# Adaptive modulation of the first 512 channels ahead of the rest, with its sums on TensorE, and the setup's pieces, transfers and parameters in another order

## The chip, the core and the metric

The kernel runs on one core of one Trainium2 chip. Its engines are TensorE (PE; its weight loads are shown apart as PEld), VectorE (DVE), ScalarE (ACT), GpSimd (POOL) and SyncE (SP, which here only issues transfers). The metric is the device time of one execution in microseconds, lower is better. All times below are of the program as a whole or offsets from the start of the profiled execution.

## The reference, cut to what matters here

```python
c_act = jax.nn.silu(c)                                          # (1, 1024)
shift, scale, gate = jnp.split(c_act @ w_ada[l] + b_ada[l], 3, axis=-1)
h = rms_norm(x, norm_w[l]) * (1.0 + scale[:, None, :]) + shift[:, None, :]
proj = h @ w_in[l]                                              # (2048, 1024) @ (1024, 8768)
# ... gated causal depthwise convolution of 31 taps, LayerNorm; latent attention of 8 heads;
# merge by sigmoid gates, w_out, residual, RMSNorm
```

Everything is float32: x is 2048 tokens by 1024 channels, `w_ada` 1024 by 3072. The change concerns `shift`, `scale` and `h`, that is, what must be there before the first large product can start.

## The kernel before

Four phases follow each other: front, value, attention, output. Only the first 117 us of the front phase are touched. There `h` is built, transposed (channels on partitions, tokens along the row), and split into a high part `h_hi` and a remainder `h_lo`, since every large product is done as three matmuls (`split3`, L52 to L54). The 2048 tokens are four chunks (g = 0 to 3) of 512, the 1024 channels eight tiles (t = 0 to 7) of 128. One **piece** is one (g, t): four 128x128 transposes on TensorE (`turn_x`, L911), the eviction `x * gain + shift` on ScalarE (`turn_out`, L429), the cast to `h_hi` (L695) and the subtraction to `h_lo` (L697) on VectorE, and then six matmuls of 512 columns on TensorE, for the first two column tiles of `w_in` at once. 32 pieces run in the order g outer, t inner. `X_BANKS` names the PSUM bank of each piece's transposes; TensorE turns piece n + 4 after the matmuls of piece n, with a hole after pieces 4 to 7, because banks are still taken (pieces 8 to 11 are turned together after piece 7).

Ahead of the first piece stand `shift` and `gain`. Their 2048 columns of `w_ada` come in four blocks of 512 (j = 0, 1 shift, j = 2, 3 scale), 2 MB each in two halves. For each block VectorE does 8 operations (L669, L672) that multiply the rows by silu(c) and add them up, and `ada_products` (L892) sums over the partitions on TensorE by 8 matmuls of one column against a constant matrix. After all four blocks VectorE makes `shift` and `gain` in four small operations (L683 to L690), and ScalarE, which waits for them (`ada_vec`), can evict the first piece.

x arrives in four groups of four row tiles. For each, ScalarE squares four tiles (`square_x`, L418) and takes the root (L422), VectorE inverts (`invert_x`, L657), GpSimd scales the four tiles (`scale_x`, L581), and TensorE may turn. The squares of later groups stand behind the evictions of pieces 0 to 11, the inversions behind pieces 3, 7 and 11. The two column tiles of `w_in` are split on ScalarE (L411) and GpSimd (L586). When a chunk's pieces are done, ScalarE evicts the two results (`evict`, L434), for g = 0 to 2 between later pieces. After piece 31 ScalarE and GpSimd split column tile 2, and TensorE goes on with it.

All input transfers are on SyncE's queue in this order: c; x group 0; blocks 0 and 1 of `w_ada`; seven small rows of parameters and the 31 x 1024 taps of the convolution (into `prm` and `taps`); `w_in` tiles 0 and 1; blocks 2 and 3; x groups 1 to 3. TensorE turns the parameters (L923, L925) after the products of block 1.

## Time and profile before

| what | us |
|---|---|
| median of 3 runs (2698.75 to 2700.75) | 2699.91 |
| the profiled execution | 2704.03 |
| its span, first to last instruction | 2702.2 |
| TensorE busy in it | 2586.2 (96%) |
| VectorE busy in it | 1755.0 (65%) |
| mean granted TensorE clock | 0.984 |

The times are of one profiled execution, 4.1 us above the median of the runs. "PE busy" counts matmuls in flight. The granted clock is 1.00 at 2.4 GHz and 0.50 at 1.2 GHz; before TensorE's clock first changes in this execution the column reads 1.00 whatever the level was, and the durations of the matmuls tell the level. In timeline rows "x16" counts matmul records: a float32 product of one column leaves two records, one of the 8 per block each.

### The profile page before, as it was taken

The page shows a single profiled execution, that of the slowest core. Times are in us where ns is not written, and L with a number is a line of the kernel's source. Part 1 is how long each engine was busy: PE and PEld are TensorE (multiplying, and loading weights), DVE is VectorE, ACT ScalarE, POOL GpSimd, SP SyncE. Part 2 cuts the span into 40 slices and gives each one's busy share as a digit, 9 for nine tenths or more (in the row PEclk, how much of TensorE's full clock was granted, in tenths as well). Part 3 has the DMA queues.
Part 4 walks back from the last instruction along what each step waited for, and adds up shares of the span by engine and source line. Part 5 has one row for each costly group of instructions (what it writes and reads, how often), then busy time and mean ns, then how long its engine had stood idle before and what let it go on. Part 6 is the DMA issues. An engine that isn't in the chain of part 4 may idle for free. (4 is left out here: it accounts for less than half of the span.)

```text
span 2702.2 us, 32620 instructions
## 1 busy us (share of the span) xinstructions
PE 2586.2 (96%) x12186; PEld 2127.4 (79%) x12186; DVE 1755.0 (65%) x2073; ACT 850.5 (31%) x1683; POOL 640.9 (24%) x592
## 2 busy tenths in 40 slices
PE   4989999999999999997899999999999999999998
PEld 4767888888888888786677877877878778888887
DVE  5777967979779789564277667667677622223442
ACT  3432111111111111232255555555555520201221
POOL 3132111111111111232032232232232320323422
PEclk8999999999999999999899999999999999999999
DMA  8053212122112121376923112112112164666542
GB/s 298 8 164 116 78 47 78 47 67 83 53 55 78 47 78 48 124 243 240 278 73 107 62 60 107 62 60 107 61 61 86 55 202 156 205 215 211 190 149 78
DMA packets 200833, 306.74 MB, mean 114 GB/s; under 512 B 18234, under 2 KB 119678, under 8 KB 190621
## 3 DMA queue, kind: packets, MB, share of 16 engines
q1 hardware_dynamic: 194604, 284.89, 32.1%
q0 software_dynamic: 6128, 20.45, 2.4%
q8 instruction: 70, 1.15, 0.2%
q14 instruction: 31, 0.25, 0.0%
HBM read 202.01 MB, written 103.28 MB: 113 GB/s over the span
## 5 line engine op out<-in xcount | busy, mean ns | idle before, releaser
L52 PE MATMUL ps_proj<-h_hi,w_hi 128*128 128x512 f32 x1696 | 670.6, 395 | 9.0 <-DVE h_lo L697 6.8
L54 PE MATMUL ps_proj<-h_hi,w_lo 128*128 128x512 f32 x1696 | 663.1, 391 | 0.0
L53 PE MATMUL ps_proj<-h_lo,w_hi 128*128 128x512 f32 x1696 | 663.0, 391 | 0.0
L812 DVE SCALAR_TENSOR_TENSOR acc<-u,taps_t,acc 128x2048 f32<-128x2048 f32 x240 | 629.0, 2621 | 8.5
L52 PEld LDWEIGHTS ps_proj<-h_hi,w_hi 128*128 128x128 f32 x1696 | 320.7, 189 | 77.9 <-issue 8.0
L53 PEld LDWEIGHTS ps_proj<-h_lo,w_hi 128*128 128x128 f32 x1696 | 320.7, 189 | 67.9 <-issue 2.5
L54 PEld LDWEIGHTS ps_proj<-h_hi,w_lo 128*128 128x128 f32 x1696 | 320.2, 189 | 67.4
L586 POOL TENSOR_TENSOR w_lo<-raw,w_hi 128x1024 fp32r<-128x1024 f32 x53 | 168.4, 3177 | 808.5 <-ACT w_hi L411 808.4
L1719 POOL TENSOR_SCALAR prob<-prob,rinv 128x512 f32<-128x512 f32 (+2 forms) x320 | 199.0, 638 | 352.3 <-DVE rinv L1670 352.1
L1675 DVE TENSOR_TENSOR pt_lo<-ps_t,pt_hi 128x512 fp32r<-128x512 f32 (+1 forms) x320 | 194.1, 609 | 96.8 <-ACT pt_hi L1594 93.1
L1594 ACT ACTIVATE pt_hi<-ps_t 128x512 fp32r<-128x512 f32 (+1 forms) x320 | 169.4, 532 | 237.6 <-PE ps_t L1500 237.6
L1652 DVE TENSOR_REDUCE nmax<-ps_ring 128x1 f32<-128x512 f32 (+3 forms) x288 | 174.6, 622 | 96.1 <-PE ps_ring L1485 78.0
L539 ACT ACTIVATE lat<-ps_proj 128x512 f32<-128x512 f32 x128 | 76.3, 598 | 493.6 <-PE ps_proj L54 429.2
L2005 DVE TENSOR_TENSOR o_y<-o_ps,o_g 128x512 f32<-128x512 f32 x64 | 43.9, 690 | 265.2 <-PE o_ps L54 201.2
L1586 ACT ACTIVATE prob<-ps_ring,nbias 128x512 f32<-128x512 f32 (+2 forms) x320 | 195.3, 625 | 37.5 <-DVE nbias L1658 33.1
L52 PE MATMUL o_ps<-o_a_hi,o_w_hi 128*128 128x512 f32 x512 | 199.8, 390 | 3.4 <-DVEq L1996 3.4
L53 PE MATMUL o_ps<-o_a_lo,o_w_hi 128*128 128x512 f32 x512 | 199.9, 390 | 0.0
L54 PE MATMUL o_ps<-o_a_hi,o_w_lo 128*128 128x512 f32 x512 | 199.8, 390 | 0.0
L1500 PE MATMUL ps_t<-ident,prob 128*128 128x128 f32 x1088 | 173.3, 275 | 14.9 <-POOL prob L1719 9.5
L1500 PEld LDWEIGHTS ps_t<-ident,prob 128*128 128x128 f32 x1088 | 131.4, 141 | 48.2 <-POOL prob L1719 12.2
L1515 PE MATMUL ps_o<-pt_hi,v_hi 128*128 128x512 f32 (+1 forms) x320 | 141.4, 442 | 0.7 <-DVE bg L1683 0.7
L1480 PE MATMUL ps_ring<-kn_hi,qn_hi 128*128 128x512 f32 (+2 forms) x320 | 125.3, 392 | 8.4 <-ACT prob L1586 5.0
(220 smaller groups left out, 4037.8 us busy)
## 6 DMA issues: line engine op xcount, KB each, us to landing
qlat<-qlat_dram SPq DMA_DIRECT2D x32, 1024.0 KB, 5.9
raw<-in_w_in_dram SPq DMA_DIRECT2D x52, 512.0 KB, 6.4
under_h<-in_w_ada_dram SPq DMA_DIRECT2D x8, 1024.0 KB, 11.2
ga_dram<-lat SPq DMA_DIRECT2D x8, 1024.0 KB, 5.0
gb_dram<-lat SPq DMA_DIRECT2D x8, 1024.0 KB, 5.0
agate_dram<-lat SPq DMA_DIRECT2D x8, 1024.0 KB, 5.0
conv_dram<-acc SPq DMA_DIRECT2D x8, 1024.0 KB, 3.9
bgate_dram<-lat SPq DMA_DIRECT2D x8, 1024.0 KB, 5.0
```

The costliest lines, as they stand in the source:

```text
L52: pe.matmul(out, wh, xh, start=first, stop=False)
L53: pe.matmul(out, wh, xl, start=False, stop=False)
L54: return pe.matmul(out, wl, xh, start=False, stop=last)
L586: pool.tensor_tensor(weights(tile)[1][:], raw[tile % 2][:], weights(tile)[0][:].bitcast(F32), ALU.subtract).then_inc(lo_made, 1)
L812: dve.scalar_tensor_tensor(acc[:], u[:, n:n + S], tap(n), acc[:], ALU.mult, ALU.add).then_inc(conv_tap if n < TAPS - 1 else conv_done, 1)
L1500: mm = pe.transpose(ps_t[:, n % 2, b * P:(b + 1) * P], prob[:, x:x + P], k.ident[:])
L1515: pe.matmul(out, v_hi[:, j, :], mh, start=(j == 0), stop=False)
L1586: act.activation(prob[:, x:x + width], ps[:, chunk_no[n, c] % RING, 0:width], ACT.Exp, bias=nbias[:, n:n + 1], accum_out=rsum[:, n, c:c + ...
L1594: act.activation(pt_hi[n % SLOTS][:, s], ps_t[:, n % 2, s], ACT.Copy).then_inc(t_hi, 1)
L1652: ins = dve.tensor_reduce(to, ps[:, chunk_no[n, c] % RING, 0:width], AX.X, ALU.max, negate=True)
L1675: dve.tensor_tensor(pt_lo[n % SLOTS][:, s], ps_t[:, n % 2, s], pt_hi[n % SLOTS][:, s].bitcast(F32), ALU.subtract).then_inc(t_lo, 1)
L1719: pool.tensor_scalar(prob[:, x:x + width], prob[:, x:x + width], rinv[:, n:n + 1], 1.0, ALU.mult, ALU.mult).then_inc(normed, 1)
```

## The change

It touches seven things in the front phase; nothing behind piece 31 differs.

1. Blocks of `w_ada` are taken in the order `ADA_COLS` = 0, 2, 1, 3: shift and scale of channels 0 to 511 first. Each half has a semaphore of its own.
2. For the first two blocks TensorE does the whole sum (`modulate`): 32 matmuls per block, each with 128x128 weights out of `w_ada` as it was loaded and one column of silu(c). The last two blocks keep the way of before, VectorE's part of them being put behind pieces 3 and 7, TensorE's (`ada_products`) behind the transposes after piece 3 and behind piece 7.
3. `shift` and `gain` are made in two halves (`shift_and_gain`), the second behind block 3.
4. `PIECES`: (0, 0 to 3), (1, 0 to 3), (0, 4 to 7), (1, 4 to 7), then chunks 2 and 3 as before. Piece 8 is the first that needs the second half of `gain`. `X_BANKS`, the squares, evictions and inversions are given by new tables.
5. VectorE scales two of four row tiles of x groups 2 and 3.
6. The small parameters and the taps are issued by GpSimd, and TensorE waits for all of them before the sums.
7. SyncE's order: c, x 0, block 0, `w_in` tiles 0 and 1, block 1, x 1, blocks 2 and 3, x 2 and 3.

```diff
-    X_BANKS = [[1, 5, 2, 6], [3, 7, 2, 6], [0, 4, 3, 7], [1, 5, 0, 4]]
+    ADA_COLS = [0, 2, 1, 3]
+    PIECES = ([(g, t) for half in range(2) for g in range(2) for t in range(half * KH, (half + 1) * KH)]
+              + [(g, t) for g in range(2, NC_) for t in range(KT)])
...
+    INVERT_AT = {3: 1, 10: 2, 16: 3}
...
+                for r, n, src in rows[1:]:
+                    pool.dma_start(prm[r:r + n, :], src.rearrange("o (t p) -> (o t) p", p=P)).then_inc(params_in, 16)
+                pool.dma_start(taps, k.conv_w.rearrange("o t c -> (o t) c")).then_inc(params_in, 16)
...
-                    for i in range(g * QB, (g + 1) * QB):
+                    for i in range(g * QB, (g + 1) * QB)[:QB // 2 if g > 1 else QB]:
...
+                def piece(n):
+                    g, t = PIECES[n]
...
+                    if n in INVERT_AT:
+                        invert_x(INVERT_AT[n])
+                        if INVERT_AT[n] > 1:
+                            scale_x(INVERT_AT[n])
...
+                shift_and_gain(0)
+                for n in range(KH):
+                    piece(n)
+                modulation(2)
+                for n in range(KH, 2 * KH):
+                    piece(n)
+                modulation(3)
+                shift_and_gain(1)
+                for n in range(2 * KH, N_PIECE):
+                    piece(n)
...
+                def modulate(j):
+                    for kh in range(2):
+                        pe.wait_ge(ada_in[j][kh], 16)
+                        for m in range(QB):
+                            for t in range(KH):
+                                at = kh * KH + t
+                                mm = pe.matmul(ps_ada[:, ADA_COLS[j] * QB + m:ADA_COLS[j] * QB + m + 1],
+                                               wada_at[j][kh][:, t, m * P:(m + 1) * P], k.cact[:, at:at + 1],
+                                               start=(at == 0 and m == 0), stop=(at == KT - 1 and m == QB - 1))
+                    mm.then_inc(ada_mm, 1)
...
-                ada_products(0)
-                for n in range(AHEAD):
-                    turn_x(n)
-                ada_products(1)
+                pe.wait_ge(cact_done, 1)
                 pe.wait_ge(params_in, 16 * len(rows))
...
-                ada_products(2)
-                ada_products(3)
+                modulate(0)
+                for n in range(AHEAD):
+                    turn_x(n)
+                modulate(1)
...
-                    held = n < KT and n >= KT - AHEAD
-                    if n == KT - 1:
-                        for m in range(KT, KT + AHEAD):
+                    if n == KH - 1:
+                        for m in range(KH, 2 * KH):
                             turn_x(m)
-                    elif not held and n + AHEAD < N_PIECE:
+                        ada_products(2)
+                    if n == 2 * KH - 1:
+                        ada_products(3)
+                    if KH <= n < N_PIECE - AHEAD:
                         turn_x(n + AHEAD)
```

TensorE before, from the second block's products on (`mean_mat` is the constant matrix, `lat` holds VectorE's sums, `ident` marks a transpose):

```order
L892 MATMUL ps_proj<-mean_mat,lat 128x1 x7
L923 MATMUL ps_proj<-ident,prm 128x68 [waits params_in]
L925 MATMUL ps_proj<-ident,lat 128x31 x8
L892 MATMUL ps_proj<-mean_mat,lat 128x1 [waits ada_step]
L892 MATMUL ps_proj<-mean_mat,lat 128x1 x7
```

and TensorE of the change, from the start of the phase (`cact` is silu(c), `under_h` where `w_ada` lands):

```order
L953 MATMUL ps_proj<-ident,prm 128x8 [waits c_in,consts]
L957 MATMUL ps_proj<-ident,prm 128x68 [waits params_in,cact_done]
L959 MATMUL ps_proj<-ident,lat 128x31 x8
L920 MATMUL ps_proj<-cact,under_h 128x1 [waits ada_in00]
L920 MATMUL ps_proj<-cact,under_h 128x1 x15
L920 MATMUL ps_proj<-cact,under_h 128x1 [waits ada_in01]
L920 MATMUL ps_proj<-cact,under_h 128x1 x15
L948 MATMUL ps_proj<-ident,u 128x128 [waits x_scaled]
```

The parameters moved to the front, and each of the first two blocks has 32 one-column matmuls where it had 8.

TensorE around the fourth piece (n = 3). Before, piece 3, the turning of piece 7, piece 4:

```order
L54 MATMUL ps_proj<-h_hi,w_lo1 128x512
L911 MATMUL ps_proj<-ident,u 128x128 [waits full_done]
L911 MATMUL ps_proj<-ident,u 128x128
L911 MATMUL ps_proj<-ident,acc 128x128 x2
L52 MATMUL ps_proj<-h_hi,w_hi0 128x512 [waits h_lo_done]
```

and in the change, where `under_h0` holds x group 1:

```order
L54 MATMUL ps_proj<-h_hi,w_lo1 128x512
L948 MATMUL ps_proj<-ident,under_h0 128x128 [waits params_sb,x_scaled]
L948 MATMUL ps_proj<-ident,under_h0 128x128 x3
L948 MATMUL ps_proj<-ident,under_h0 128x128 [waits full_done,x_scaled]
L948 MATMUL ps_proj<-ident,under_h0 128x128 x3
L948 MATMUL ps_proj<-ident,under_h0 128x128 [waits full_done,x_scaled]
L948 MATMUL ps_proj<-ident,under_h0 128x128 x3
L948 MATMUL ps_proj<-ident,under_h0 128x128 [waits full_done,params_sb,x_scaled]
L948 MATMUL ps_proj<-ident,under_h0 128x128 x3
L929 MATMUL ps_proj<-mean_mat,lat 128x1 [waits ada_step]
L929 MATMUL ps_proj<-mean_mat,lat 128x1 x7
L52 MATMUL ps_proj<-h_hi,w_hi0 128x512 [waits h_lo_done]
```

Between pieces 3 and 4 now stand 16 transposes that wait for the scaled x group 1, and 8 products that wait for VectorE's sums of block 2.

VectorE around its fourth piece. Before:

```order
L697 TENSOR_TENSOR h_lo<-wada_gate,h_hi 128x512 [waits h_hi_done]
L657 RECIPROCAL ss<-ss 128x4 [waits root_done]
L695 CAST h_hi<-wada_gate 128x512 [waits full_done]
L697 TENSOR_TENSOR h_lo<-wada_gate,h_hi 128x512 [waits h_hi_done]
L695 CAST h_hi<-wada_gate 128x512 [waits full_done]
```

and in the change:

```order
L705 TENSOR_TENSOR h_lo<-wada_gate,h_hi 128x512 [waits h_hi_done]
L664 RECIPROCAL ss<-ss 128x4 [waits root_done]
L679 TENSOR_SCALAR lat<-under_h0,cact 128x512 [waits ada_in21,ada_in20]
L679 TENSOR_SCALAR lat<-under_h0,cact 128x512
L682 SCALAR_TENSOR_TENSOR lat<-under_h0,cact,lat 128x512 [waits ada_step] x6
L703 CAST h_hi<-wada_gate 128x512 [waits full_done]
```

The eight operations of block 2 now stand between VectorE's pieces 3 and 4.

## Rows read from the trace of the kernel before

**Rows 1.** Busy time per stretch: each engine's, then granted clock, DMA share, GB/s
```profile
core 0: us, PE busy (x) PEld busy (x) DVE busy (x) ACT busy (x) POOL busy (x), PEclk, DMA share, GB/s
28.00:32.00 4.00, 3.81 (x31) 3.62 (x29) 0.65 (x1) 1.61 (x2) 3.37 (x2) 1.00 1.05 399
32.00:36.00 4.00, 0.00 (x0) 0.00 (x0) 1.39 (x3) 0.00 (x0) 1.27 (x1) 0.61 1.05 386
80.00:84.00 4.00, 3.82 (x12) 3.12 (x13) 3.22 (x7) 1.99 (x3) 0.00 (x0) 0.59 0.02 4
```
**Rows 2.** Timeline of TensorE: start, duration, what; in brackets idle before and releaser
```profile
20.17 3.57 PE L892 MATMUL ps_proj<-mean_mat,lat 128*128 128x1 f32 x16 [17.65 <-DVE lat L672]
25.51 0.69 PE L911 MATMUL ps_proj<-ident,u 128*128 128x128 f32 x2 [1.77 <-POOL acc L581]
...
28.98 2.10 PE L892 MATMUL ps_proj<-mean_mat,lat 128*128 128x1 f32 x16
...
31.13 0.68 PE L925 MATMUL ps_proj<-ident,lat 31*128 31x31 f32 x8
...
44.94 3.57 PE L892 MATMUL ps_proj<-mean_mat,lat 128*128 128x1 f32 x16 [1.83 <-DVE lat L672]
51.41 0.76 PE L52 MATMUL ps_proj<-h_hi,w_hi 128*128 128x512 f32 x1 [2.91 <-DVE h_lo L697]
...
80.18 0.50 PE L52 MATMUL ps_proj<-h_hi,w_hi 128*128 128x512 f32 x1 [2.48 <-DVE h_lo L697]
...
86.92 0.60 PE L911 MATMUL ps_proj<-ident,under_h 128*128 128x128 f32 x4
87.28 0.48 PE L52 MATMUL ps_proj<-h_hi,w_hi 128*128 128x512 f32 x1
...
88.75 0.60 PE L911 MATMUL ps_proj<-ident,under_h 128*128 128x128 f32 x4
...
110.91 0.38 PE L911 MATMUL ps_proj<-ident,part 128*128 128x128 f32 x2
...
117.92 1.99 PE L957 MATMUL ps_proj<-acc,mean_mat 128*128 128x512 f32 x4 [1.14 <-POOL w_lo L586]
```
**Rows 3.** Timeline of VectorE, blocks of `w_ada`, `gain`, an inversion, and two later operations
```profile
15.26 0.88 DVE L669 TENSOR_SCALAR lat<-under_h,cact 128x512 f32<-128x512 f32 x2 [15.26 <-DMA under_h<-in_w_ada_dram]
...
20.64 2.32 DVE L669 TENSOR_SCALAR lat<-under_h,cact 128x512 f32<-128x512 f32 x2 [0.43 <-DMA under_h<-in_w_ada_dram]
22.88 5.76 DVE L672 SCALAR_TENSOR_TENSOR lat<-under_h,cact,lat 128x512 f32<-128x512 f32 x6
...
40.82 4.06 DVE L672 SCALAR_TENSOR_TENSOR lat<-under_h,cact,lat 128x512 f32<-128x512 f32 x6
48.62 0.17 DVE L683 SCALAR_TENSOR_TENSOR shift<-ps_proj,prm_t 128x8 f32<-128x8 f32 x1 [3.74 <-PE ps_proj L892]
...
56.60 0.18 DVE L657 RECIPROCAL ss<-ss 128x4 f32<-128x4 f32 x1 [0.21 <-ACT ss L422]
...
115.67 3.28 DVE L713 TENSOR_SCALAR u<-u,freqs 128x2048 f32<-128x2048 f32 x1
...
130.55 1.23 DVE L719 TENSOR_SCALAR u<-u 128x2048 f32<-128x2048 f32 x1
```
**Rows 4.** Timeline of GpSimd: scaling of x group 0, and its first transfer
```profile
20.30 2.37 POOL L581 TENSOR_SCALAR u<-u,ss 128x1024 f32<-128x1024 f32 x2 [17.81 <-DVE ss L657]
22.66 2.80 POOL L581 TENSOR_SCALAR acc<-acc,ss 128x1024 f32<-128x1024 f32 x2
...
143.77 1.12 POOL L595 DMA_DIRECT2D u<-in_w_ada_dram  x1 [0.72 <-DMA trig_dram<-u]
```
**Rows 5.** Timeline of ScalarE, the first eviction
```profile
49.30 0.78 ACT L429 ACTIVATE wada_gate<-ps_proj,shift,gain 128x512 f32<-128x512 f32 x1 [19.06 <-DVE gain L690]
```
**Rows 6.** Timeline of SyncE's queue, the taps
```profile
13.05 0.25 SPq L334 DMA_DIRECT2D lat<-in_conv_w_dram  x1
```
**Rows 7.** DMA from 20 to 28 us, in 40 slices of 0.2 us
```profile
GB/s 312 233 207 169 202 202 159 128 54 41 23 38 123 97 105 187 292 361 328 333 317 302 156 77 28 20 10 20 23 20 23 31 172 123 92 61 110 317 338 420
```

More of the change, by code:

```diff
@@ L196, in front_phase @@
         params_in = sem("params_in")
-        ada_in = [sem(f"ada_in{j}") for j in range(ADA_J)]
+        ada_in = [[sem(f"ada_in{j}{kh}") for kh in range(2)] for j in range(ADA_J)]
         x_in = [sem(f"x_in{g}") for g in range(NC_)]
@@ L297, in _ @@
             def _(sp):
-                def row(r, n, src, landed):
-                    sp.dma_start(prm[r:r + n, :], src.rearrange("o (t p) -> (o t) p", p=P)).then_inc(landed, 16)
                 def load_x(g):
@@ L326, in store_part @@
                     sp.dma_start(dst[1], part_lo.bitcast(F32)).then_inc(part_lo_out, 16)
-                row(*rows[0], c_in)
+                sp.dma_start(prm[R_C:R_C + KT, :], k.c.rearrange("o (t p) -> (o t) p", p=P)).then_inc(c_in, 16)
                 load_x(0)
                 ada(0)
-                ada(1)
-                for r in rows[1:]:
-                    row(*r, params_in)
-                sp.dma_start(taps, k.conv_w.rearrange("o t c -> (o t) c")).then_inc(params_in, 16)
                 tile_weights(0)
                 tile_weights(1)
+                ada(1)
+                load_x(1)
                 ada(2)
                 ada(3)
-                for g in range(1, NC_):
-                    load_x(g)
+                load_x(2)
+                load_x(3)
                 sp.dma_start(freqs[:], k.freqs).then_inc(pos_in, 16)
@@ L688, in _, with shift_and_gain @@
-                dve.tensor_scalar_add(gain[:], gain[:], 1.0).then_inc(ada_vec, 1)
-                dve.wait_ge(ada_vec, 3)
-                dve.tensor_tensor(gain[:], gain[:], k.prm_t[:, R_NORM:R_NORM + KT], ALU.mult).then_inc(ada_vec, 1)
-                for n in range(N_PIECE):
-                    g, t = divmod(n, KT)
+                def shift_and_gain(half):
+                    t = slice(half * KH, (half + 1) * KH)
+                    of = lambda r: slice(r + half * KH, r + (half + 1) * KH)
+                    scale = float(D) if half else 1.0
+                    dve.wait_ge(ada_mm, 2 * (half + 1))
+                    dve.scalar_tensor_tensor(gain[:, t], ps_ada[:, of(KT)], scale, k.prm_t[:, of(R_BADA + KT)],
+                                             ALU.mult, ALU.add).then_inc(ada_vec, 1)
+                    dve.scalar_tensor_tensor(shift[:, t], ps_ada[:, of(0)], scale, k.prm_t[:, of(R_BADA)],
+                                             ALU.mult, ALU.add).then_inc(ada_vec, 1)
+                    dve.wait_ge(ada_vec, 4 * half + 1)
+                    dve.tensor_scalar_add(gain[:, t], gain[:, t], 1.0).then_inc(ada_vec, 1)
+                    dve.wait_ge(ada_vec, 4 * half + 3)
+                    dve.tensor_tensor(gain[:, t], gain[:, t], k.prm_t[:, of(R_NORM)], ALU.mult).then_inc(ada_vec, 1)
@@ L896, in turn_x @@
                 def turn_x(n):
-                    g, t = divmod(n, KT)
-                    b = X_BANKS[g][t % 4]
-                    if t == 0:
-                        pe.wait_ge(x_scaled, QB * (g + 1))
-                        if g == 1:
-                            pe.wait_ge(ada_vec, 2)
-                            pe.wait_ge(params_sb, 2)
-                        if g >= 2:
-                            pe.wait_ge(chunk_out, 2 * (g - 1))
-                    before = [m for m in range(n) if X_BANKS[m // KT][m % 4] == b]
+                    g, t = PIECES[n]
+                    b = X_BANKS[n]
+                    pe.wait_ge(x_scaled, QB * (g + 1))
+                    if b == 7:
+                        pe.wait_ge(params_sb, 2)
+                    if b == 3:
+                        pe.wait_ge(ada_vec, 6)
+                    if n >= 2 * KT and b % NC_ < 2:
+                        pe.wait_ge(chunk_out, 2 * (b % NC_ + 1))
+                    before = [m for m in range(n) if X_BANKS[m] == b]
                     if before:
```

62 lines of the change are left out of this document (30 added, 32 removed).

## The prediction, made before the changed kernel had run

> **What bounds the kernel now.** TensorE is busy for 96% of the span, so a change in the first 117 us moves the end by as much as it moves the point from which TensorE runs without waiting. I read the timeline of TensorE first [rows 2], and in it the waits in brackets: the three product groups with waits ahead (17.65 us, 1.83 us), 2.91 us ahead of the first large matmul at 51.41, 2.48 us ahead of the one at 80.18. Then the engine that ends each wait: VectorE's blocks of `w_ada` [rows 3], GpSimd's scaling [rows 4], ScalarE's first eviction at 49.30 [rows 5]. I call that moment T0, since the first `gain` ends there. Last, the granted clock by stretches [rows 1]. The reader is to see that up to T0 the sums over `w_ada` end last, and after it TensorE, which needs 1.83 us a piece with its four transposes (86.92 to 88.75). The last transposes end at 110.91 + 0.38 = 111.3, which is T0 + 62.0. Behind them follow four pieces, ScalarE's and GpSimd's split and tile 2 (the row at 117.92, [rows 2]); all of that hangs on the last piece by the same chain in both kernels, so I move it as a whole. I compare the moment at which the last transposes end, 111.3 before, and carry the difference to the end one to one.
>
> **Up to T0: what goes and what comes.** VectorE's eight operations for blocks 0 and 1 go (the second block took 2.32 + 5.76 = 8.1 us beside GpSimd, a block alone some 4.9). What comes instead is on TensorE: 32 one-column matmuls a block for 8. The price is in the row of the same form, 128x128 weights and one column: 16 records in 3.57 us at the low level of the clock (20.17 and 44.94), 2.10 at 28.98, when the clock had mostly risen [rows 2]. Four such groups back to back are 14.0 us at the low level and 7.0 at the high one.
>
> When can the first begin? Block 0 was complete at 15.26 [rows 3]; at 386 GB/s [rows 1] its second megabyte takes 2.7 us, so its first half is there at 12.5. But TensorE now first waits for all parameters. GpSimd is free from 20.30 - 17.81 = 2.5 us [rows 4]. It issues eight transfers, each between 0.25 us (SyncE's price of the taps, [rows 6]) and 1.12 (GpSimd's for 512 KB, [rows 4]): done between 4.5 and 11.5. Landing is the unknown. Where the taps were in flight before, the stream fell to 10 to 31 GB/s for eight slices on end, 1.6 us [rows 7]; at 20 GB/s the taps' 127 kB are 6.3 us. So the parameters are there between 7 and 20 us. I take 13.5, near the middle, since GpSimd has nothing else to do. With 0.9 us for turning them (0.68 for the taps at 31.13, and one transpose more), the sums start at 14.4; bounds 13.4 and 20.9.
>
> The Trainium skill (DMA: Bandwidth & Descriptors, "Why a DMA increments its semaphore by 16 and not by 1") says that the number of DMA engines of a transfer must divide its slowest dimension, which for 31 rows is one engine, and that GpSimd's software path gives some copies all 16 nevertheless. By the first the taps land late (the rival below), by the second early; rows 7 fit the first for SyncE's queue, and no row shows GpSimd's.
>
> First block: 14.4 + 14.0 = 28.4. Transposes of pieces 0 to 3: 3.5 us at the low level (25.51 to 28.98), 31.9. Scaled x is there at 25.5 at the latest. Second block: before, the clock was high from the end of these transposes (the faster group at 28.98) to 32.9 (mean 0.61 in 32 to 36, [rows 1]), 3.9 us. If it does the same again, 3.9 us do the work of 7.8 and the other 6.2 go at the low level: 10.1 us, 42.0. If not, 45.9. From the last product to the first eviction 49.30 - 48.51 = 0.8 (44.94 + 3.57 = 48.51). **T0 is 42.8 instead of 49.3, a lead of 6.5 us.**
>
> The Trainium skill (TensorE: Matmul & The Clock Gate, "Part 4: PE-mode transpose") says that transposes don't count as work that raises the clock. Here the clock rose right behind 3.5 us of nothing but transposes, so the row speaks against it; by the page the lead would be 2.6 us.
>
> The transfers' new order by itself gives nothing: block 1 was complete at 20.64 [rows 3], and 1.05 MB of `w_in` ahead of it, even at the 156 GB/s that are the mean of rows 7, add 6.7: it is there before the second block's sums start at 31.9.
>
> **From T0 on: 62.0 us before.** Pieces 0 to 3 are as before up to the inversion, which ends at T0 + 7.5 (56.60 + 0.18 - 49.30). Then GpSimd scales x group 1 and VectorE does block 2. That very pair stood at 20.30: GpSimd took 5.2 us and VectorE 8.1 [rows 3, 4]. So x 1 is scaled at 12.7 and block 2 summed at 15.6. TensorE is through with four pieces at about 9.8 and waits; before, it had pieces 4 to 7 to work on in this time. Sixteen transposes: 3.5 us at the low level, 16.2; products of block 2: 19.7 (both at the high level: 17.4). I take the low level, as an idle of 2.48 us ahead of 80.18 was enough for 0.59 in 80 to 84 [rows 1, 2].
>
> Pieces 4 to 7 with three turnings: 4 x 1.83 - 0.46 = 6.9, and 1.7 more for a start at the low level as long as the one at 80 to 84, 3.3 us of 4 [rows 1]: 28.3. Block 3 on VectorE is hidden: 15.6 + 4 x 1.15 + 4.9 = 25.1. Its products take 1.9, `gain` 0.8: ScalarE's piece 8 can start at T0 + 31.0. Its first matmul is 2.1 later (51.41 - 49.30), 33.1. Pieces 8 to 27, twenty of 1.83, are 36.6: 69.7. The half scaling on VectorE comes twice, behind pieces 10 and 16: two operations of 1024, alone 0.6 each, beside GpSimd up to 1.6 (2048 took 1.23 and 3.28, [rows 3]), in a stretch where VectorE needs 1.15 of the 1.83 us anyway. Each also waits for the root and its partner on GpSimd. I take 4 us of TensorE's waits for both (bounds 1 and 7), and 0.9 for the clock after the idle ahead of piece 8. **Sum: 74.6, that is 12.6 more than before**; bounds 67 (no low level, no waits) and 78.
>
> In all 12.6 - 6.5 = **+6.1 us**. The profiled execution of 2704.03 would be 2710.1; put on the median of the runs, 2699.91, it is 2706.0.
>
> **Rivals.** (1) *The clock rises inside the first block's sums.* Then 4.0 us at the low level, 5.0 at the high one, transposes 1.8 and the second block 7.0: T0 = 33.0, a lead of 16.3, and the products in the second half are shorter by 3.3: 9.3 - 16.3 = -7.0, 2692.9, faster. It decides as soon as the rise comes before the middle of the first block. Against it: the group at 44.94 was done at the low level, 1.83 us behind another of its kind, and after the group at 28.98 the clock was low by 32.9. For it: no row has such matmuls for more than 3.6 us on end. The Trainium skill (TensorE: Matmul & The Clock Gate, "Part 1: The HAM clock gate") has sustained matmuls raise the clock and makes no exception for one-column ones; this rival is what it would give. 12%.
> (2) *The taps are late.* Parameters at 20 us, sums from 20.9, 6.5 later than taken: 2712.5. For it rows 7, against it that GpSimd's queue need not spread like SyncE's. 27%.
> (3) *The waits after T0 are mostly covered.* Sum 67 to 69 instead of 74.6, the change then within 2 us of nothing: about 2699. It needs the scaling and block 2 to interleave better than the pair at 20.30 did. 18%.
> (4) *The transposes don't raise the clock for the second block.* T0 = 46.7, 2709.9. 10%.
> The forecast, lead 6.5 and 12.6 given back, has 33%, with a range of its own from 2701 to 2711.
>
> **How the numbers follow.** 0.2% is 5.4 us, about what a measurement of this kernel can tell. Slower than 2705.3: over half of the forecast's case, nearly all of (2) and (4), together 0.55. Faster than 2694.5: most of (1), a little of (3), 0.12. Between: 0.33. The range leaves out the far half of (1) below, and (2) with the upper bound of the waits above: 2694 to 2717.
>
> **What would show it.** Right: the one-column matmuls of the first block spread over about 14 us with a start near 14; the first eviction at 40 to 44; TensorE idle for some 3 us behind piece 3 and again ahead of piece 8; VectorE's block 2 taking 8 us; waits ahead of the matmuls of pieces 11 and 17; the transposes' end at 114 to 120. Wrong: a first block done in 9 us or less (rival 1), a start of the sums near 20 (rival 2), pieces 4 to 7 right behind piece 3 (rival 3). The whole would be wrong if something behind piece 31, where nothing is changed, took up or gave back what the first 117 us lose.

## The result: 8.9 us slower, by the mechanism that was forecast

| | before | changed |
|---|---|---|
| median of the runs (7 each, same chip) | 2699.91 us (2698.66 to 2703.29) | 2708.92 us (2702.73 to 2716.21) |
| ratio to before, 95% interval | | 1.0033 [1.0023, 1.0043] |
| profiled execution, its span | 2704.03, 2702.2 us | 2710.15, 2708.3 us |
| first eviction, T0 [rows 5] | 49.30 | 41.07 |
| end of the last transposes [rows 2] | 111.3 | 118.8 |
| first matmul of tile 2 [rows 2] | 117.92 | 125.42 |
| from there to the end of the span | 2584.3 | 2582.9 |

The 8.9 us are the ratio to before, put on 2700 us; the two medians differ by 9.0. TensorE starts 8.2 us earlier on the large products and is 7.5 us late when the last x is turned. The 1.4 us that come back behind it can't be read as an effect of the change: that code is the same in all fourteen kernels of this study, and it took between 2579.7 and 2586.0 us in their profiled executions.

### The changed kernel up to T0

TensorE's timeline of the changed kernel (columns as in [rows 2]; x64 are the matmul records of one block's sum):

```profile
11.44 0.35 PE L957 MATMUL ps_proj<-ident,prm 68*128 68x68 f32 x1 [8.72 <-DMA lat<-in_conv_w_dram]
11.71 1.06 PE L959 MATMUL ps_proj<-ident,lat 31*128 31x31 f32 x8
12.70 13.81 PE L920 MATMUL ps_proj<-cact,under_h 128*128 128x1 f32 x64
...
28.97 0.56 PE L948 MATMUL ps_proj<-ident,u 128*128 128x128 f32 x2
29.37 0.38 PE L948 MATMUL ps_proj<-ident,acc 128*128 128x128 f32 x2
29.59 10.77 PE L920 MATMUL ps_proj<-cact,under_h 128*128 128x1 f32 x64
43.19 0.77 PE L52 MATMUL ps_proj<-h_hi,w_hi 128*128 128x512 f32 x1 [2.83 <-DVE h_lo L705]
```

The first block is the low level from end to end: 13.81 us for 64 records is 0.216 us each, against 0.223 in [rows 2] at 44.94. The transposes behind it go from 0.63 us to 0.38 a pair at 29, and the second block has some 3 us at the high level. GpSimd issues the parameters in 0.51 to 0.73 us each, the taps last, at 5.96, and these are there at 11.4. The stretch of 10 to 31 GB/s [rows 7] is gone: from 20 to 28 us the stream stays at 386 to 388 GB/s. Busy time per stretch (columns as in [rows 1]), first before, then changed:

```profile
20.00:24.00 4.00, 3.57 (x16) 3.48 (x16) 3.56 (x5) 0.00 (x0) 3.69 (x4) 1.00 0.74 180
24.00:28.00 4.00, 2.49 (x12) 2.49 (x13) 4.00 (x6) 0.51 (x1) 1.46 (x1) 1.00 0.56 133
```
```profile
20.00:24.00 4.00, 4.00 (x20) 4.00 (x21) 0.00 (x0) 0.00 (x0) 4.00 (x3) 1.00 1.05 386
24.00:28.00 4.00, 4.00 (x20) 4.00 (x21) 0.00 (x0) 0.00 (x0) 0.76 (x1) 1.00 1.05 388
```

### The changed kernel behind T0

ScalarE's first eviction, T0, and TensorE again, the interruptions of its pieces:

```profile
41.07 0.78 ACT L431 ACTIVATE wada_gate<-ps_proj,shift,gain 128x512 f32<-128x512 f32 x1 [21.56 <-DVE gain L697]
```
```profile
54.29 3.68 PE L948 MATMUL ps_proj<-ident,under_h 128*128 128x128 f32 x16 [3.89 <-POOL under_h L588]
57.76 3.41 PE L929 MATMUL ps_proj<-mean_mat,lat 128*128 128x1 f32 x16
...
70.69 1.84 PE L929 MATMUL ps_proj<-mean_mat,lat 128*128 128x1 f32 x16
74.08 0.66 PE L948 MATMUL ps_proj<-ident,u 128*128 128x128 f32 x2 [1.56 <-ACT wada_gate L431]
...
96.83 0.50 PE L52 MATMUL ps_proj<-h_hi,w_hi 128*128 128x512 f32 x1 [2.15 <-DVE h_lo L705]
```

VectorE, block 2 beside GpSimd's scaling of x 1 (which took 5.59 us from 48.65), and the second half of `gain`:

```profile
40.48 0.16 DVE L690 SCALAR_TENSOR_TENSOR gain<-ps_proj,prm_t 128x4 f32<-128x4 f32 x1 [24.41 <-PE ps_proj L920]
...
48.47 1.75 DVE L679 TENSOR_SCALAR lat<-under_h,cact 128x512 f32<-128x512 f32 x2
50.14 6.62 DVE L682 SCALAR_TENSOR_TENSOR lat<-under_h,cact,lat 128x512 f32<-128x512 f32 x6
...
72.56 0.16 DVE L690 SCALAR_TENSOR_TENSOR gain<-ps_proj,prm_t 128x4 f32<-128x4 f32 x1 [6.78 <-PE ps_proj L929]
```

And the granted clock after each interruption (third column from the end, as in [rows 1]):

```profile
56.00:60.00 4.00, 4.00 (x22) 4.00 (x20) 3.90 (x9) 2.80 (x5) 0.00 (x0) 0.50 0.00 0
60.00:64.00 4.00, 4.00 (x14) 3.31 (x15) 3.97 (x8) 0.80 (x2) 0.00 (x0) 0.50 0.01 4
...
76.00:80.00 4.00, 4.00 (x12) 3.17 (x12) 3.13 (x7) 3.97 (x8) 0.97 (x1) 0.50 0.71 264
...
96.00:100.00 4.00, 3.17 (x11) 2.63 (x12) 3.86 (x7) 1.55 (x2) 0.23 (x1) 0.70 0.01 4
```

VectorE stands idle for 24.41 us ahead of T0, from 16.1 to 40.5; before, it had done three of its four blocks by 39.5. Its two blocks are left for a time when it is wanted for the pieces. From the end of piece 3 to the start of piece 4 TensorE now passes 10.6 us (50.4 to 61.04) with a wait, transposes and products, and from the end of piece 7 to the start of piece 8 another 4.5 (70.69 to 75.18). That is where the lead goes, and e3_sums_early below tests it.

### The profile page after: what moved, and what is told of

Its sections match the earlier page's. It is cut to its first block and busy times, and to the rows that moved or that the text cites. A ratio compares the mean times of both kernels' runs of the same rounds, so it can differ in the third digit from the quotient of the medians.

```text
span 2708.3 us, 32825 instructions
## 1 busy us (share of the span) xinstructions
PE 2610.1 (96%) x12282; PEld 2150.1 (79%) x12282; DVE 1746.1 (64%) x2065; ACT 851.1 (31%) x1683; POOL 642.4 (24%) x596
## 5 line engine op out<-in xcount | busy, mean ns | idle before, releaser
L1538 PEld LDWEIGHTS ps_t<-ident,prob 128*128 128x128 f32 x1088 | 132.1, 142 | 48.1 <-POOL prob L1757 12.2
```

The source lines that it names most:

```text
L1538: mm = pe.transpose(ps_t[:, n % 2, b * P:(b + 1) * P], prob[:, x:x + P], k.ident[:])
```

## The experiments

Each was timed together with the kernel before on the same chip: 10 to 12 runs each, 7 of e12_gpsimd_only and 5 of e11_both. "Last turned" is the end of the last transposes, "stretch" is from T0 to there, both in the profiled execution; the last column is (ratio - 1) x 2700 us. The intervals are some 2.5 us to each side, so differences between two rows below about 3.5 us are not shown by them (below 4 to 5 us for the two kernels with fewer runs). T0 is of a single execution: eight of the kernels (the changed one and e3, e4, e6, e7, e9, e11 and e12) are the same up to the first block's sums, and these began anywhere from 12.70 to 14.12 us, so T0 can differ by 1.4 us without any effect of an edit.

| kernel | T0 | last turned | stretch | ratio to before | us to before |
|---|---|---|---|---|---|
| before | 49.30 | 111.3 | 62.0 | 1 | 0 |
| changed | 41.07 | 118.8 | 77.7 | 1.0033 [1.0023, 1.0043] | +8.9 |
| e1_params | 48.48 | 108.4 | 59.9 | 1.0000 [0.9991, 1.0009] | 0.0 |
| e8_split_late | 45.65 | 107.4 | 61.7 | 0.9989 [0.9980, 0.9998] | -3.0 |
| e2_params_back | 41.65 | 115.8 | 74.2 | 1.0023 [1.0013, 1.0032] | +6.2 |
| e5_sums_vector | 39.93 | 116.5 | 76.6 | 1.0016 [1.0007, 1.0025] | +4.3 |
| e10_split_held | 36.13 | 110.3 | 74.2 | 0.9999 [0.9989, 1.0009] | -0.3 |
| e3_sums_early | 44.41 | 109.9 | 65.5 | 1.0004 [0.9995, 1.0013] | +1.1 |
| e6_three_vector | 36.65 | 112.6 | 76.0 | 1.0001 [0.9992, 1.0010] | +0.3 |
| e9_x1_first | 35.22 | 105.1 | 69.9 | 0.9987 [0.9977, 0.9998] | -3.5 |
| e4_scale_pool | 41.77 | 116.1 | 74.4 | 1.0027 [1.0017, 1.0036] | +7.3 |
| e7_scale_early | 37.42 | 107.7 | 70.3 | 0.9998 [0.9989, 1.0007] | -0.5 |
| e12_gpsimd_only | 35.76 | 103.8 | 68.1 | 0.9971 [0.9960, 0.9982] | -7.8 |
| e11_both | 35.87 | 100.2 | 64.3 | 0.9957 [0.9943, 0.9970] | -11.6 |

### e1_params and e8_split_late: what the parameters' queue gives

> The kernel before, with one thing of the change: the small parameters and the 31 rows of taps are issued by GpSimd instead of SyncE. If the taps in SyncE's queue caused the stretch of 10 to 31 GB/s ahead of blocks 2 and 3, that stretch goes, blocks 2 and 3 land some 5 us sooner, the first eviction comes at 43 to 45 instead of 49.3, and nothing is given back behind it, since VectorE's blocks then end last and TensorE has its pieces in the old order: 5 to 6 us less than before, about 2694. Rival: the dip is not what ends last (VectorE beside GpSimd is): first eviction at 48 to 49.3, within 1.5 us of before.

```diff
-                for r in rows[1:]:
-                    row(*r, params_in)
-                sp.dma_start(taps, ...).then_inc(params_in, 16)
...
+                for r, n, src in rows[1:]:
+                    pool.dma_start(prm[r:r + n, :], ...).then_inc(params_in, 16)
+                pool.dma_start(taps, ...).then_inc(params_in, 16)
```

Missed: no gain that can be seen. The transfers did come sooner (VectorE's block 2 no longer waits for its data), but T0 moved by 0.8 us only. VectorE of e1_params, and under it GpSimd:

```profile
21.70 2.31 DVE L669 TENSOR_SCALAR lat<-under_h,cact 128x512 f32<-128x512 f32 x2 [0.46 <-DMA under_h<-in_w_ada_dram]
23.93 9.95 DVE L672 SCALAR_TENSOR_TENSOR lat<-under_h,cact,lat 128x512 f32<-128x512 f32 x6
33.80 0.87 DVE L669 TENSOR_SCALAR lat<-under_h,cact 128x512 f32<-128x512 f32 x2
```
```profile
21.35 2.38 POOL L581 TENSOR_SCALAR u<-u,ss 128x1024 f32<-128x1024 f32 x2 [14.46 <-DVE ss L657]
23.71 2.80 POOL L581 TENSOR_SCALAR acc<-acc,ss 128x1024 f32<-128x1024 f32 x2
26.48 5.53 POOL L586 TENSOR_TENSOR w_lo<-raw,w_hi 128x1024 fp32r<-128x1024 f32 x2
```

With `w_in` landing earlier too, GpSimd's split now follows its scaling without a pause, and block 1 on VectorE takes 12.2 us where it took 8.1 [rows 3] and takes 4.9 alone. What the earlier transfer gave was lost where it started GpSimd's split beside VectorE. e8_split_late takes that away:

> The kernel before with the parameters on GpSimd's queue (as in e1_params), and with GpSimd's split of the first two column tiles of w_in held back until VectorE has done all four blocks. In e1_params VectorE's block 1 took 2.31 + 9.95 = 12.2 us beside 10.7 us of GpSimd (scaling and split), where before it took 8.1 beside the scaling alone, and the blocks alone take 4.9. Theory (the two engines slow each other, and this ate what the earlier transfers gave): block 1 takes about 8.1, the first eviction comes 4 us sooner than in e1_params, at 44 to 45; the split then ends some 2 us ahead of the first large matmul and costs nothing: 4 to 5 us less than before, about 2695.5. Rival (block 1 is slow for its data, not for GpSimd): first eviction still at 48, same time as before, or later if the split comes late.

```diff
                 scale_x(0)
+                pool.wait_ge(ada_step, KT * ADA_J)
                 split_lo(0)
```

```profile
21.38 2.31 DVE L670 TENSOR_SCALAR lat<-under_h,cact 128x512 f32<-128x512 f32 x2 [0.45 <-DMA under_h<-in_w_ada_dram]
23.61 5.76 DVE L673 SCALAR_TENSOR_TENSOR lat<-under_h,cact,lat 128x512 f32<-128x512 f32 x6
30.38 0.88 DVE L670 TENSOR_SCALAR lat<-under_h,cact 128x512 f32<-128x512 f32 x2 [1.01 <-DMA under_h<-in_w_ada_dram]
```

Block 1 is back at 8.1 us and T0 comes 2.8 us sooner than in e1_params (4 were expected: block 2 now waits 1 us to land, and one of `gain`'s operations took 0.74 us beside the split). The time is 3.0 us less than before. By block 1's duration and by T0 the theory of the two engines holds; in the runs the 3.0 us to e1_params are within the noise of the two rows. The parameters' queue and the held split are worth about 3 us together (0.5 to 5.4 by the interval), the queue alone nothing that shows. (The held split alone was not tried.)

### e2_params_back, e5_sums_vector, e10_split_held: what sets T0 in the changed kernel

> The changed kernel with the small parameters and the taps back on SyncE's queue, behind block 1, and turned by TensorE behind the second block's sums instead of ahead of the first. Theory: ahead of the first eviction TensorE's one-column matmuls at the low level end last, not the transfers, so the place of the parameters is worth only about 1 us there: first eviction 40.5 to 43, time within 2 us of the changed kernel. Rival: the changed kernel lives on the early taps and the stream without a dip: blocks 2 and 3 and x 1 land 5 us later and the waits behind piece 3 grow, 3 to 5 us slower than the changed kernel.

```diff
                 ada(1)
+                for r, n, src in rows[1:]:
+                    sp.dma_start(prm[r:r + n, :], ...).then_inc(params_in, 16)
+                sp.dma_start(taps, ...).then_inc(params_in, 16)
                 load_x(1)
...
-                for r, n, src in rows[1:]:
-                    pool.dma_start(prm[r:r + n, :], ...).then_inc(params_in, 16)
-                pool.dma_start(taps, ...).then_inc(params_in, 16)
```

TensorE's wait for the parameters and their transposes go behind `modulate(1)`. T0 came as expected, at 41.65. The time, 2.7 us less than the changed kernel, is more than the 2 us that were expected, but the intervals don't tell it from none; the rival, 3 to 5 us slower, is out. In the changed kernel the parameters' queue gives nothing that shows, and waiting for them costs 1.1 us ahead of the sums (these start at 11.59 here, when their data is there, and at 12.70 there).

> The changed kernel with the sums of its first two blocks back on VectorE (8 operations a block, then 8 one-column matmuls on TensorE), everything else kept: order of channels, halves of gain, pieces, queues. Theory: 64 one-column matmuls per block in 13.8 and 10.8 us at the low level are what sets the first eviction at 41.1; with VectorE's 4.9 us a block behind the landing (block 1 lands at about 27 to 28) it comes at 33 to 36, and the stretch behind it stays 76 to 79 us, since blocks 2 and 3 are there or land soon: 5 to 7.5 us less than the changed kernel, about 2702. Rival: transfers or GpSimd's part end last then (x 1, blocks 2 and 3 not landed when the pieces want them), the stretch behind the first eviction grows by what is won: within 1.5 us of the changed kernel.

```diff
+                modulation(0)
+                modulation(1)
                 shift_and_gain(0)
...
-                modulate(0)
+                ada_products(0)
...
-                modulate(1)
+                ada_products(1)
```

Half a miss: 4.6 us less than the changed kernel where 5 to 7.5 were expected, but T0 moved by 1.1 us only, and of the profiled difference 2.3 us stand ahead of the last transposes' end; the rest is behind piece 31, where the code is the same. Block 0 on VectorE met GpSimd's scaling and split, and took 12.2 us (2.29 + 9.93), just as in e1_params. With the split held back until both blocks are summed (the diff is against e5_sums_vector):

> e5_sums_vector (VectorE sums the first two blocks, all else as in the changed kernel) with GpSimd's split of the first two column tiles of w_in held back until VectorE has done both. In e5_sums_vector VectorE's block 0 took 2.29 + 9.93 = 12.2 us beside GpSimd's 10.7 us of scaling and split. Theory: it takes 8.1 beside the scaling alone, block 1 follows at once, the first eviction comes at 35 to 36 instead of 39.9; the split is done by 35 and holds nothing up: 4 to 5 us less than e5_sums_vector, about 2700.5, and 8 less than the changed kernel. Rival: what stands behind the first eviction (x 1, block 2) does not move with it, at most 1.5 us less than e5_sums_vector.

```diff
                 scale_x(0)
+                pool.wait_ge(ada_step, 2 * KT)
                 split_lo(0)
```

As expected: VectorE took 2.29 + 5.76, T0 came at 36.13, and the kernel needs 9.2 us less than the changed one, 4.6 less than e5_sums_vector. So sums on TensorE at the low level are not dear against VectorE beside a busy GpSimd (T0 1.1 us apart), and are dear (5 us) against VectorE with the split out of the way. The first two blocks' sums on VectorE, with the split held, turn the change from a loss into no difference that shows. The stretch is still 74.2 us where the kernel before had 62.0: the interruption is there as in the changed kernel, and the earlier T0 pays for it.

### e3_sums_early, e6_three_vector, e9_x1_first: what the interruption of the pieces costs

> The changed kernel with VectorE's sums of blocks 2 and 3 ahead of the first half of gain, where VectorE was idle for 24 us, both products of TensorE behind the transposes that follow piece 3, blocks 2 and 3 ahead of x 1 in SyncE's queue, and the second half of gain behind piece 7. Theory (the interruption of the pieces by blocks 2 and 3 costs what the lead had brought): the wait of 3.9 us behind piece 3 shrinks to below 1.5, block 3's products no longer stand between piece 7 and piece 8, first eviction still at 41 to 42, the last transposes end some 6 to 7 us sooner than the changed kernel's 118.8, so 6 to 7.5 us less than the changed kernel, about 2702. Rival: x 1 (scaled by GpSimd after the inversion) ends that wait anyway and the pieces are bound by their own chain: at most 1 to 2 us less.

```diff
-                load_x(1)
                 ada(2)
                 ada(3)
+                load_x(1)
...
-                shift_and_gain(0)
-                for n in range(KH):
-                    piece(n)
                 modulation(2)
-                for n in range(KH, 2 * KH):
-                    piece(n)
                 modulation(3)
+                shift_and_gain(0)
+                for n in range(2 * KH):
+                    piece(n)
                 shift_and_gain(1)
...
                         ada_products(2)
-                    if n == 2 * KH - 1:
                         ada_products(3)
```

The total came about as expected (7.8 us less than the changed kernel, where 6 to 7.5 were named), in another split. The stretch behind T0 fell by 12.2 us, from 77.7 to 65.5; but T0 was 3.3 us later, since this time the clock did not rise behind the transposes and the second block's sums took 13.65 us:

```profile
30.12 13.65 PE L918 MATMUL ps_proj<-cact,under_h 128*128 128x1 f32 x64
46.52 0.77 PE L52 MATMUL ps_proj<-h_hi,w_hi 128*128 128x512 f32 x1 [2.75 <-DVE h_lo L705]
...
56.44 2.25 PE L946 MATMUL ps_proj<-ident,under_h 128*128 128x128 f32 x16 [1.73 <-POOL under_h L588]
58.52 3.65 PE L927 MATMUL ps_proj<-mean_mat,lat 128*128 128x1 f32 x32
```

Ahead of x 1's transposes TensorE now waits 1.73 us instead of 3.89, and there is no stop ahead of piece 8. TensorE's named waits in the stretch, leaving out the one for the first piece, are 3.7 us (1.73 and 1.98 ahead of piece 17) where the changed kernel had 7.6 (3.89, 1.56, 2.15). Much of the rest of the 12.2 us is the clock: from 56 us on its mean over 4 us was never below 0.75 here, and in the changed kernel it was 0.50 from 56 to 64, 0.64 in 64 to 68 and 0.50 in 76 to 80. Single executions differ in that, but the 7.8 us are of all runs.

This is the experiment that settles the verdict: the same pieces in the same order, the same sums on TensorE, VectorE's two blocks done while it was idle, and no loss that shows (+1.1 us; by the interval between 1.4 less and 3.5 more than before). Two things had to move with the blocks: their transfers go ahead of x 1's, and block 3's products stand behind piece 3 with block 2's. How the gain divides between the three was not tried.

> e3_sums_early with TensorE's whole sum kept for block 0 only: VectorE sums blocks 1 and 2 ahead of the first half of gain, and block 3 two operations at a time behind the casts of pieces 0 to 3; TensorE does block 2's products behind piece 3 and block 3's behind the transposes that follow. Theory (in e3_sums_early the second block's 13.65 us of one-column matmuls at the low level ended last before the first eviction at 44.4, and VectorE stood idle from 16.5 to 30): VectorE does block 1 from about 25 to 30, while GpSimd is done, and the first eviction comes at 35 to 36.5; the rest of the chain, from the transposes of piece 4 on, moves by what x 1 allows, 7 to 8 us: about 2694. Rival: x 1's squares, root and scaling don't come forward (landing of x 1 behind block 3, at about 41.5) and take the place of the wait: first eviction at 36, but no more than 3 us less than e3_sums_early, about 2699.

Against e3_sums_early:

```diff
-                modulation(2)
-                modulation(3)
+                modulation(1)
+                modulation(2)
                 shift_and_gain(0)
                 for n in range(2 * KH):
                     piece(n)
+                    if n < KH:
+                        modulation(3, [n])
...
-                modulate(1)
+                ada_products(1)
...
                     if n == KH - 1:
+                        ada_products(2)
                         for m in range(KH, 2 * KH):
                             turn_x(m)
-                        ada_products(2)
```

The rival was right: 0.8 us less than e3_sums_early. T0 came at 36.65, but ScalarE of this kernel shows what took its place:

```profile
36.65 0.78 ACT L431 ACTIVATE wada_gate<-ps_proj,shift,gain 128x512 f32<-128x512 f32 x1 [15.21 <-DVE gain L697]
42.04 1.06 ACT L420 ACTIVATE lat<-under_h 128x1024 bf16<-128x1024 f32 x1 [4.61 <-DMA under_h<-in_x_dram]
43.00 0.19 ACT L420 ACTIVATION_READ_ACCUMULATOR lat<-under_h 128x1 f32 x1
43.09 0.76 ACT L431 ACTIVATE wada_gate<-ps_proj,shift,gain 128x512 f32<-128x512 f32 x1
```

The first square of x 1 stands behind the first eviction on ScalarE, waits for its data, and the second eviction waits with it. With x 1 ahead of block 3:

> e6_three_vector with x 1 ahead of block 3 in SyncE's queue, and VectorE's sum of block 3 in one piece behind the casts of piece 3 and the inversion. In e6_three_vector the first eviction came at 36.65, but ScalarE's first square of x 1, which stands right behind it, waited 4.61 us for x 1 to land and held up the next eviction, and x 1 was scaled at 55.2 only. Theory: x 1 lands at about 36.5, the four evictions and squares run through (36.7 to 43.5), x 1 is scaled at 49 to 50, block 3 is summed by 52, its products end by 56; from the transposes of piece 4 (at 55.46 in e6_three_vector) on all is 5 to 6 us sooner: about 2695. Rival: VectorE's sum of block 3 beside GpSimd's scaling (8.3 and 5.6 us) and the products behind it hold up pieces 4 to 8 by as much as x 1 gains: within 2 us of e6_three_vector.

```diff
                 ada(2)
-                ada(3)
                 load_x(1)
+                ada(3)
...
-                    if n < KH:
-                        modulation(3, [n])
+                    if n == KH - 1:
+                        modulation(3)
```

TensorE turned x 1 at 48.80 instead of 55.46, 6.7 us sooner; the profiled execution was 7.1 us shorter (2694.3 against 2701.4), the ratio 3.8 us. The theory held in the trace; in the runs the size was below it and barely clear of the noise. 1.4 of the 6.7 us are T0's (35.22 against 36.65), most of it from the start of the first sums (13.07 against 14.12), which no edit moved.

### e4_scale_pool, e7_scale_early, e12_gpsimd_only, e11_both: scaling on VectorE

> The changed kernel with all scaling of x 2 and x 3 on GpSimd, as before the change. In the changed kernel VectorE's two half scalings took 2.29 us each and TensorE waited 2.15 us ahead of piece 17, none ahead of piece 11. Theory: that wait goes and none takes its place (the groups are scaled 1 us later by GpSimd, but wanted later still): 1.5 to 3 us less than the changed kernel, about 2706. Rival: GpSimd's four operations alone take 4.4 us instead of 3.5 and x 2's transposes wait for them: same as the changed kernel or slower by 1.

```diff
-                    for i in range(g * QB, (g + 1) * QB)[:QB // 2 if g > 1 else QB]:
+                    for i in range(g * QB, (g + 1) * QB):
...
-                        if INVERT_AT[n] > 1:
-                            scale_x(INVERT_AT[n])
```

TensorE's wait ahead of piece 17 went from 2.15 to 0.86 us. The time, 1.6 us less, is as expected, but too small to be told from none.

> e6_three_vector with the squares of x 2 and x 3 behind pieces 4 to 7 and 10 to 13, the inversions behind pieces 7 and 13, and all scaling on GpSimd. Theory: the waits of about 2 us ahead of pieces 11 and 17 (1.98 and 2.15 us of TensorE ahead of piece 17, from VectorE's scaling) go: 2 to 3 us less than e6_three_vector, about 2691.5. Rival: VectorE's own pace of casts, or ScalarE with more squares between evictions, gives new waits of the same size: within 1 us of e6_three_vector.

```diff
-    SQUARES_AT = {..., 7: [8], 8: [9], 9: [10], 10: [11], 13: [12], 14: [13], 15: [14], 16: [15]}
+    SQUARES_AT = {..., 4: [8], 5: [9], 6: [10], 7: [11], 10: [12], 11: [13], 12: [14], 13: [15]}
...
-    INVERT_AT = {3: 1, 10: 2, 16: 3}
+    INVERT_AT = {3: 1, 7: 2, 13: 3}
```

The diff is against e6_three_vector, together with that of e4_scale_pool. 0.8 us less than e6_three_vector by the ratios: the rival, or a gain too small to see. (The profiled executions are 5.4 us apart, 2696.03 against 2701.40; the medians of the runs, 2700.24 and 2700.94, don't bear that out.)

> e9_x1_first with what e7_scale_early changes: squares of x 2 and x 3 behind pieces 4 to 7 and 10 to 13, inversions behind pieces 7 and 13, all scaling on GpSimd. Theory: TensorE waited 1.96 us ahead of piece 17 in e9_x1_first, from VectorE's scaling; that wait goes, and e7_scale_early against e6_three_vector (0.7 us less) shows that little takes its place: 1 to 2 us less than e9_x1_first, about 2695.5, 4 to 5 us less than before. Rival: the scaling on VectorE costs nothing that can be measured: within 1 us of e9_x1_first.

The diff is that of e7_scale_early on e9_x1_first, so again both the squares and the engine that scales. 8.1 us less than e9_x1_first, and 11.6 less than before, the fastest kernel of the study; I had expected 1 to 2. Twelve runs of e9_x1_first spread from 2690.86 to 2707.14, five of e11_both from 2685.10 to 2690.13. The profiled executions show what differs in them. TensorE's stretches of e9_x1_first, and then of e11_both:

```profile
52.00:56.00 4.00, 4.00 (x17) 3.86 (x18) 3.85 (x11) 2.59 (x4) 0.00 (x0) 0.50 0.58 138
56.00:60.00 4.00, 4.00 (x14) 3.18 (x13) 0.29 (x1) 1.10 (x2) 0.00 (x0) 0.55 0.00 0
84.00:88.00 4.00, 4.00 (x15) 3.21 (x14) 2.66 (x7) 1.55 (x2) 0.00 (x0) 0.64 0.02 4
```
```profile
52.00:56.00 4.00, 4.00 (x27) 3.70 (x26) 3.01 (x6) 4.00 (x8) 0.00 (x0) 0.88 0.61 146
56.00:60.00 4.00, 4.00 (x24) 3.39 (x23) 2.84 (x9) 2.47 (x5) 2.59 (x3) 1.00 0.01 2
```

The first had low clock for most of 8 us behind x 1's transposes and again behind the wait ahead of piece 17 (1.96 us, where e11_both has one of 1.60 and stayed at 1.00 behind it). e12_gpsimd_only stands between the two:

> e9_x1_first with all scaling on GpSimd, and the squares and inversions left where they are (behind pieces 7 to 10 and 13 to 16). It stands between e9_x1_first (0.9987 of before) and e11_both (0.9957 of before), which was 8 us less where 1 to 2 were expected. Theory: the engine that scales is worth 1 to 2 us, as between e4_scale_pool and the changed kernel, about 2695; what e11_both has beyond that comes from the earlier squares, or from stretches at the low clock that its executions happened not to have. Rival: VectorE's scaling, with the wait and the low clock behind it, is worth all of it: 2690 to 2691, as e11_both.

Its diff is that of e4_scale_pool on e9_x1_first. 4.3 us less than e9_x1_first, 3.8 more than e11_both: between the theory and the rival. Its profiled execution shows the wait ahead of piece 17 at 0.86 us and the clock at 1.00 in 84 to 88, where e9_x1_first had 1.96 and 0.64; behind x 1's transposes the clock was as low as there, 0.50 from 52 to 60. Moving the scaling back to GpSimd gives part and the earlier squares perhaps the rest, but the interval of e12_gpsimd_only [0.9960, 0.9982] overlaps both neighbours', so only the whole step from e9_x1_first to e11_both is shown. How much of it is the clock that happened to stay high in the executions timed stays open.

## Why the prediction was right, step by step

The forecast was 2706.0 us and slower; 2708.92 was measured, inside the forecast case's own range. Of the places where it said to look, most showed what it named: the first block's matmuls over 13.81 us, T0 at 41.07, 3.89 us idle behind piece 3, block 2 in 8.4 us, a wait ahead of piece 17, the transposes' end at 118.8. Two did not: ahead of piece 8 the idle was 1.56 us and not some 3, and ahead of piece 11 there was none.

- **Sums on TensorE.** 14.0 and 10.1 us were put in, 13.81 and 10.77 measured. Rival 1, a clock that rises inside the first block, is out: in all nine kernels that have it, the changed one and eight of the experiments, it took 13.79 to 13.81 us. The Trainium skill (TensorE: Matmul & The Clock Gate, "Part 1: The HAM clock gate") says that activity of the engine releases the lower clock, which would have given that rival; in these nine blocks no rise came.
- **Parameters.** Taken at 13.5, measured 11.44; rival 2 is out. GpSimd's issues cost 0.51 to 0.73 us each and were done at 6.5, between the bounds of 4.5 and 11.5. The taps landed 5.3 us after they were issued, where 6.3 had been estimated for their slow stream; but the small rows, of 1 to 12 KB, took 4.5 to 5.2 us as well, so the landing was not a matter of the taps' size. The bounds were not well worked out: their own terms end at 17.8 (11.5 and 6.3) and not at 20, and the earliest start of the sums was put at 13.4, behind both the landing of block 0's first half at 12.5 and 0.9 us of turning, though early parameters would be turned while that half is on its way. The sums started at 12.70, below that bound. With it T0 came at 41.07 instead of 42.8, a lead of 8.2 instead of 6.5.
- **Clock behind the transposes.** Assumed to rise as in [rows 2], and it did, for about 3 us where 3.9 were taken (10.77 us where all-low took 13.65); but that it did was in part luck, as e3_sums_early shows. Rival 4 (10%) had a better chance than that: of the fourteen profiled executions, the clock rose in the first transposes or in the one-column matmuls right behind them in six (before, the changed kernel, e1_params, e2_params_back, e4_scale_pool, e12_gpsimd_only) and not in the other eight. (The low clock by 32.9 in [rows 1] speaks less against rival 1 than the prediction has it: TensorE had been idle there since 31.8.)
- **Block 2 beside the scaling.** 5.2 and 8.1 us from [rows 3, 4], measured 5.59 and 1.75 + 6.62 = 8.4. x 1 was turned from T0 + 13.2 (12.7 put in), products of block 2 done at T0 + 20.1 (19.7). Rival 3, that the waits are covered, is out by these rows.
- **Piece 8.** Its eviction was put at T0 + 31.0 and came at 32.1 (73.16); its first matmul at T0 + 34.1 (33.1).
- **The waits for scaled x and the clock, the mis-sized terms.** 4 us were taken for pieces 11 and 17 and 0.9 for the clock. Measured: no wait ahead of piece 11 and 2.15 ahead of piece 17. But from piece 8's first matmul at 75.18 to 118.8 are 43.6 us; less 36.6 for twenty pieces and the 2.15, 4.9 are left, and nearly all of it is clock: it was at a mean of 0.50 in 76 to 80 and 0.93 in 80 to 84, and at 0.70 and 0.87 in the two stretches from 96 to 104, which together with the time from 75.18 comes to some 4.4 us. So the waits were 1.9 us less than put in and the clock 4.0 more: the term was too small although the waits were too large in it. The stretch was 77.7 us where 74.6 were put in (1.0 us of the difference ahead of piece 8, 2.1 behind), at the upper bound of 78.
- **Behind piece 31.** The first matmul of tile 2 moved by the same 7.5 us as the last transposes. What follows differs by up to 6 us between single executions with the same code, so it neither confirms nor denies the one to one. That the profiled execution took 2710.15 us where 2710.1 were forecast is luck: it is the 7.5 us less the 1.4 behind.
- **The range.** Its upper end, 2717, is 1 us more than rival 2 and the upper bound of the waits give together (2712.5 + 3.4).

Lead 8.2, given back 15.7: +7.5 us where it was counted, against +6.1 forecast. The lead was put 1.7 us too small and the loss 3.1, and these cancelled in part.

What the prediction did not say is what the idle VectorE was worth. It has no term for VectorE's 24 idle us, while they are where blocks 2 and 3 could have gone: e3_sums_early, 7.8 us.

## What to carry over

When an engine is relieved ahead of the critical point and loaded behind it, look for the idle time that it now has: work that is only late because of where it stands in the program's order (and whose data can be there in time) can go back there; that was worth 7.8 us, about as much as the whole lead of 8.2. A transfer that lands earlier may start work on another engine that slows the critical one (VectorE's block 1 in e1_params, 12.2 us for 8.1), so hold that work back before judging the transfer. On an engine that works in order, a step whose data is late holds everything written behind it, however ready (ScalarE's 4.61 us in e6_three_vector).

## What the runs showed of the hardware

**VectorE and GpSimd slow each other.** One block of `w_ada` took VectorE 4.9 us alone, 8.1 beside four scalings and 12.2 beside four scalings and two splits. GpSimd's six operations took 10.7 us there (2.38 + 2.80 + 5.53) and 9.1 in e3_sums_early with VectorE idle (2.22 + 2.20 + 4.65). Together they were through in 12.5 us, where 4.9 + 9.1 are 14.0: little better than one after the other. The Trainium skill (SBUF — State Buffer, "SBUF: two separate sides") says that the two share a port pair, which an operation of GpSimd, or one of VectorE with two inputs in SBUF or in certain modes, holds for the whole instruction while the other fully blocks. By this the pair would take nearly the sum; the 12.5 us come near the 14.0 and are 1.5 less.

**One-column matmuls.** 64 records stood back to back for 13.8 us, TensorE without a gap, and the clock stayed at 1.2 GHz in all nine kernels that have them ahead of the first transposes. Within the sixteen transposes that follow, it rose to 2.4 GHz in the changed kernel (0.63 to 0.38 us a pair). In e2_params_back it rose only behind all sixteen, when one-column matmuls ran again: 10.54 us for the second block. The Trainium skill (TensorE: Matmul & The Clock Gate, "Part 4: PE-mode transpose") has it that transposes don't raise the clock; the rise in these rows speaks against it, though it came in six executions of fourteen.

**The same wait, another clock.** Before had 2.48 us of idle ahead of 80.18 and a mean clock of 0.59 behind it [rows 1, 2]; e1_params had 2.28 us at the same place and no fall. Spreads of 5 to 16 us between runs of one kernel would fit such stretches that come or don't, which no experiment here separates. A difference of 2 us between two single executions should not be read as an edit's.
